# A two-layer encoder on one core: output product of the 1024-token requests in f16 parts, product with V one head later, side work in other slots, loops written out

## The chip, the cores and the metric

One Trainium2 chip, and of it one core. The time is device microseconds of one launch; three runs of the kernel before are given by their median. One further execution was profiled; all rows of the trace are from it, and its times count from the span's start.

## The reference, cut to what matters

Two requests, a prompt of 512 tokens and a sample of 1024, go through the same trunk of two layers with shared weights (`D_MODEL` = 1024, everything in float32). One layer does, for a request:

```python
h = rms_norm(x, g_norm) * (1 + scale) + shift           # scale, shift, gate from Linear(SiLU(c))
q_lat, kv_lat, k_rope, z_a, q_b, k_b, v_b, z_b = split(h @ w_in)
oa = attention(8 heads, q and k of 64 + 32 from q_lat, kv_lat, k_rope; v of 64)     # MLA
ob = attention(8 query heads, 2 key heads of 64, q and k normed per head, axial rotary)   # GQA
out = concat(oa * silu(z_a), ob * silu(z_b)) @ w_out
x = x + gate * out
```

Attention is a full softmax over all tokens of the request. After both layers comes a last RMS norm.

## The kernel before, in words

**Four instances.** The program runs layer 0 for the prompt (q = 0, r = 0), layer 0 for the sample (q = 1, r = 1), then the same for layer 1 (q = 2, 3). The instances of 512 tokens (4 tiles of 128) are called short here, those of 1024 tokens (8 tiles) long. In the code `delay` is 1 for short ones. Every engine has its own program; they meet in counting semaphores alone.

**Key phase.** An instance begins with `key_step`, one for each tile of keys and two to drain: x is loaded by SyncE into the one buffer `xn`, squared and scaled on ScalarE (the root on GpSimd), transposed on TensorE (`h^T0`, `h^T1`), modulated on VectorE into `hT`, multiplied with `Wkv` (`kv`), and the keys and values of the tile are made from it. In a long instance `h` is split into f16 parts (high on ScalarE, low on VectorE in `h_low`) and kept in memory; SyncE issues the store after `h_low` and the next x after `h^T1`. `load_w`, after the first step, brings the f16 parts of the query weights (two transfers). They were made in tiles 2 and 3 of the short instance of the same layer. `Wout` is loaded after the last step, in two transfers, and so is `gate`, one row for all partitions.

**Tiles.** Then each tile of 128 query tokens runs through 16 slots, one for each head: 0 to 7 MLA, 8 to 15 GQA. In slot h TensorE runs `turn(h)` (transposes of the exponentials of head h, L677), `scores(h + 2)` (L695), side work, and `mix`, the product with V (L905). The exponentials are split into f16 parts: ScalarE copies the transposed block to f16 (`move_pt`, L1398), VectorE subtracts to get the low part (L1214), and `mix` adds three products (high with high, high with low, low with high). In short instances `mix(h - 1)` runs in slot h, since two heads fit into `PT`; in long ones `mix(h)` runs in its own slot and waits for `pt_low` of that head. `turn(h)` waits for the exponentials of h and for the low part of head h - 1, whose PSUM banks it writes. ScalarE's order in a slot is `move_pt(h)`, the exponential of h + 1 (L1390), tanh for a z; VectorE's in a long instance is the outputs of a group of heads, low part, side result, row maximum of head h + 2 (L1197), other side results.

**Side work.** The dictionaries `FINISH`, `GATE_A`, `GATE_B`, `PREPARE`, `TURN` and `LEFT_OVER` say which side product runs in which slot, ahead of `mix` (left of the bar) or behind it; "/0" and "/1" are the two halves (four k each) of a product over 1024. For tile i: the gates z_a, z_b of the tile; y_b^T and the output product out0, out1 of tile i - 1; q_lat, q_b, q_up and the transposes of q for tile i + 1; y_a^T of the tile. A side product has one PSUM bank (`SIDE`) in a long instance, two in a short one; it starts when the product before it has been taken out by VectorE (`mm_free`). In `scores` the heads 0, 1, 4 and 8 wait for the latest side result (L695's wait is on `mm_free` of `rounds.now() - later`).

**Output product.** For both lengths `yT` is float32, and out0, out1 are eight float32 matmuls each of 128x512 (`product`, L695) with `Wout`, whose rows GpSimd has multiplied with `gate` in the slots `GATE_SLOTS` of the first tile (`gate_output_weights`). VectorE adds x (L1182). The z and q products of long instances already run as three f16 products (`product3`, L686 to L688).

**Gates.** GpSimd's `gates` turns sums of exponentials and scales into one factor per head and multiplies it into G; for long instances the factor holds `in_unscale` of the f16 products.

**Loops.** In short instances all tiles are written out. In long ones `over_tiles` writes tiles 0 and 7 out and puts tiles 1 to 6 into a hardware loop (`tile_loop`, `Fori`) on every engine, with waits on values from registers; `key_steps` does the same for the steps in the middle. In layer 1 the last norm of tile i - 1 hangs on each tile (`final_square`, `final_rstd`, `final_rows`, L1230), with a load of `g_final` and a store of the result by SyncE.

Of the kernel before, what the change touches and what calls it, by code (L numbers as in the profile page):

```python
# [18 lines left out]
F16 = mybir.dt.float16  # L19
# [67 lines left out]
def slots(first, last, ada):  # L87

    parts = [GATE_B, TURN] + ([ADA] if ada else [])
    if not first:  # L90
        parts += [GATE_A, FINISH]
    else:
        parts.append(LEFT_OVER)
    if not last:
        parts.append(PREPARE)
    return [[[n for p in parts for n in p.get(slot, "|").split("|")[a].split()] for a in (0, 1)]
            for slot in range(2 * HEADS)]
# [7 lines left out]
class Count:  # L105


    def __init__(self):
        self.n, self.over = 0, 0

    def now(self):
        return self.n + self.over
# [4 lines left out]


@contextmanager
def tile_loop(eng, first, end, by=1, **counts):  # L120

    assert (end - first) % by == 0
    with eng.Fori(first, end - by + 1, by) as i:
        at = {k: c.n for k, (c, _) in counts.items()}
        for c, per in counts.values():
            c.over = (i - first) * per
        yield i
        for k, (c, per) in counts.items():
            assert c.n - at[k] == per * by, (k, c.n - at[k], per)
            c.over = 0  # L130
            c.n += per * (end - first - by)


def encoder(nc, x_prompt, x_sample, c_prompt, c_sample, w_ada, b_ada, g_norm, w_in, g_qa, w_uq,
# [20 lines left out]
    with ExitStack() as ctx:  # L155
# [43 lines left out]
        rows1_sb = sb("rows1_sb", [32, P])  # L199
# [5 lines left out]
        w_top = sb("w_top", [P, len(W_CHUNKS)])  # L205
        w_max = sb("w_max", [P, DEPTH])
# [8 lines left out]
        hT_parts = hT[:, 0, :, :].rearrange("p k n -> p (k n)").bitcast(F16).rearrange("p (a k n) -> p a k n", a=2, k=KD)  # L215
        Wq_parts = Wq[:, :, :].rearrange("p k n -> p (k n)").bitcast(F16).rearrange("p (k n) -> p k n", k=KD)

        def w_chunk(j):
            k, n, c, w = W_CHUNKS[j]
            return Wq[:, k:k + n, c:c + w], parts[:, j % 2, :].rearrange("p (k a n) -> p k a n", k=n, a=2)  # L220
        junk = sb("junk", [P, 2 * D], BF16)
# [47 lines left out]

        g_final_rows = [region1[:, 0:D], region2[:, at - D:at]]  # L270
# [40 lines left out]
        def side_bank(S, n):  # L311
# [14 lines left out]
            "h_high", "h_low",  # L326
# [14 lines left out]
        def pt_block(h, S, c):  # L341

            return c + (h % 2 * S // P if 2 * S <= SMAX else 0)
# [17 lines left out]
        def key_steps(eng, NT, per, step, loop_from=2):  # L361


            for i in range(loop_from):
                step(i, i % 2)
            if loop_from < NT - 2:
                with tile_loop(eng, loop_from, NT - 2, by=2, **per) as i:
                    step(i, 0)
                    step(i + 1, 1)
            for i in range(max(loop_from, NT - 2), NT):  # L370
                step(i, i % 2)
            step(NT, 0)
            step(NT + 1, 1)

        def over_tiles(eng, NT, per, tile):

            tile(0, True, False)
            if NT == tiles[0]:
                for i in range(1, NT - 1):
                    tile(i, False, False)  # L380
            else:
                with tile_loop(eng, 1, NT - 1, **per) as i:
# [1305 lines left out]
```

## Time and profile before

| | us |
|---|---|
| median of three runs | 2509.02 |
| lowest, highest | 2506.0, 2953.74 |
| the profiled execution, its own time | 2508.32 |
| its span, first to last instruction | 2506.5 |
| TensorE matmul busy | 2243.5 (90%) |
| VectorE busy | 1405.4 (56%) |
| ScalarE busy | 971.3 (39%) |
| GpSimd busy | 798.9 (32%) |
| mean granted TensorE clock | 0.958 |

Busy time is the union of an engine's instructions; matmul ends are modelled and overlap the next one's start, so the pace of TensorE is better read from starts in the chain than from mean durations. The chain of the work that ended last follows each step back to what released it; "issue" in it is time in which the engine waited for nothing that the profile shows. A float32 matmul of 512 columns stands in the trace as two records. The two layers' long instances run from about 450 to 1250 and from about 1640 to 2506 us.

### The profile page before, as it was taken

How to read it: one execution, taken by the hardware profiler on the slowest of the kernel's cores; microseconds unless marked ns; L12 is line 12 of the kernel's file. 1: busy time of each engine (PE TensorE's matmuls, PEld its weight loads, DVE VectorE, ACT ScalarE, POOL GpSimd, SP SyncE). 2: the span in 40 equal slices, each digit the busy share in tenths (PEclk: the TensorE clock that was granted, in tenths of full speed). 3: DMA queues.
4: the chain of work that ended last, by engine and by line, in shares of the span. 5: the costliest groups of instructions: out<-in, count | busy, mean ns of one | idle time of the engine just before them, and what ended most of it. 6: DMA issues, size and time to landing. Idle time of an engine off the chain costs nothing.

```text
span 2506.5 us, 44027 instructions
## 1 busy us (share of the span) xinstructions
PE 2243.5 (90%) x16426; PEld 1343.1 (54%) x16426; DVE 1405.4 (56%) x2342; ACT 971.3 (39%) x2174; POOL 798.9 (32%) x1311
## 2 busy tenths in 40 slices
PE   3888998699999999999988899868998988988997
PEld 1445554355666666666544555435565655655664
DVE  3546565375665556565544655547565555545563
ACT  0123344233544444444412334422453443434452
POOL 0553231375332123112155323147532212203210
PEclk7899999799999999999999999989999999999999
DMA  9712134430000000000521001363000000010001
GB/s 297 273 43 68 59 110 163 176 151 10 18 18 8 25 17 25 8 25 17 192 94 67 18 35 71 119 232 136 10 18 27 10 35 27 9 35 27 9 26 42
DMA packets 75965, 172.29 MB, mean 69 GB/s; under 512 B 7586, under 2 KB 34312, under 8 KB 75292
## 3 DMA queue, kind: packets, MB, share of 16 engines
q1 hardware_dynamic: 75808, 170.03, 19.0%
q8 instruction: 118, 1.93, 0.3%
q14 instruction: 39, 0.32, 0.0%
HBM read 130.12 MB, written 39.90 MB: 68 GB/s over the span
## 4 chain that ended last, share of the span: by engine, by line
PE 71%; DVE 14%; issue 5%; DMA 3%; ACT 3%; POOL 2%; SPq 2%; DVEq 0%; POOLq 0%; ACTq 0%
PE psum L695 41%; PE psum L677 11%; PE psum L905 6%; DVE region L1214 4%; PE psum L686 4%; PE psum L688 4%; PE psum L687 4%; DVE nmax L1197 3%; DVE hT L1009 1%; DMA xn<-x_after_layer 1%; DMA xn<-in_x_sample 1%; POOL region L1451 1%; ACT region L1398 1%; ACT region L1374 1%; DVE region L1172 1%
## 5 line engine op out<-in xcount | busy, mean ns | idle before, releaser
L1398 ACT ACTIVATE region<-psum 128x512 f16<-128x512 f32 x640 | 354.0, 594 | 708.8 <-PE psum L677 708.7
L1214 DVE TENSOR_TENSOR region<-psum,region 128x512 f16<-128x512 f32 x640 | 416.8, 684 | 301.9 <-ACT region L1398 301.3
L677 PE MATMUL psum<-ident,region 128*128 128x128 f32 (+1 forms) x3208 | 445.2, 280 | 59.1 <-issue 35.1
L677 PEld LDWEIGHTS psum<-ident,region 128*128 128x128 f32 (+1 forms) x3208 | 364.4, 142 | 126.8 <-issue 92.2
L1197 DVE TENSOR_REDUCE nmax<-psum 128x1 f32<-128x1024 f32 (+1 forms) x384 | 399.1, 1039 | 56.2 <-PE psum L695 55.4
L695 PE MATMUL psum<-Wout,region 128*128 128x512 f32 x768 | 352.3, 604 | 3.9 <-DVE region L1182 1.6
L695 PE MATMUL psum<-KTa,region 96*128 96x512 f32 x640 | 323.5, 622 | 24.6 <-DVE region L1172 13.1
L1451 POOL TENSOR_TENSOR rsum<-sums,v_scale 128x8 f32<-128x8 f32 x48 | 13.1, 273 | 812.3 <-ACT region L1390 812.3
L1451 POOL TENSOR_TENSOR region<-region,rope_sb 128x64 f32<-128x64 f32 (+3 forms) x384 | 159.4, 436 | 308.7 <-DVE region L1168 293.6
L1390 ACT ACTIVATE region<-psum,nmax,unscale 128x1024 f32<-128x1024 f32 (+1 forms) x192 | 204.4, 1064 | 136.0 <-DVE nmax L1200 135.2
L1390 ACT ACTIVATE region<-psum,nmax 128x1024 f32<-128x1024 f32 (+1 forms) x192 | 186.9, 973 | 113.3 <-DVE nmax L1197 112.3
L695 PEld LDWEIGHTS psum<-Wout,region 128*128 128x128 f32 x768 | 143.4, 193 | 157.1 <-issue 145.2
L695 PE MATMUL psum<-Wq,hT 128*128 128x512 f32 (+1 forms) x512 | 204.6, 547 | 7.9 <-DMA hT<-h_transposed 6.5
L905 PEld LDWEIGHTS psum<-Vb,region 128*128 128x128 f16 x3840 | 138.9, 99 | 122.2 <-DVE region L1214 49.5
L905 PEld LDWEIGHTS psum<-Va,region 128*128 128x128 f16 x3840 | 136.3, 98 | 112.1 <-DVE region L1214 69.4
L686 PE MATMUL psum<-Wq,hT 128*128 128x512 f16 (+1 forms) x512 | 181.3, 354 | 6.7 <-DMA hT<-h_transposed 6.7
L905 PE MATMUL psum<-Vb,region 128*128 128x64 f16 x3840 | 154.9, 195 | 31.2 <-DVE region L1214 15.9
L687 PE MATMUL psum<-Wq,hT 128*128 128x512 f16 (+1 forms) x512 | 181.2, 354 | 0.0
L688 PE MATMUL psum<-Wq,hT 128*128 128x512 f16 (+1 forms) x512 | 181.1, 354 | 0.0
L695 PE MATMUL psum<-region,hT 128*128 128x416 f32 x384 | 153.1, 556 | 22.0 <-DVE hT L1009 19.4
L695 PE MATMUL psum<-KTb,region 128*128 128x512 f16 x640 | 170.8, 381 | 1.2 <-DVE region L1158 1.2
L695 PEld LDWEIGHTS psum<-KTa,region 96*128 96x128 f32 x640 | 112.5, 198 | 105.0 <-issue 85.5
(132 smaller groups left out, 2518.9 us busy)
## 6 DMA issues: line engine op xcount, KB each, us to landing
Wout<-in_w_out SPq DMA_DIRECT2D x8, 2048.0 KB, 9.7
w_in_parts<-parts SPq DMA_DIRECT2D x28, 512.0 KB, 3.2
Wq<-w_in_parts SPq DMA_DIRECT2D x4, 3584.0 KB, 18.4
Va<-in_w_ada SPq DMA_DIRECT2D x12, 1024.0 KB, 5.7
Wq<-in_w_in SPq DMA_DIRECT2D x6, 2048.0 KB, 14.1
hT<-h_transposed SPq DMA_DIRECT2D x24, 512.0 KB, 3.3
h_transposed<-parts SPq DMA_DIRECT2D x16, 512.0 KB, 2.7
Wq<-in_w_ada SPq DMA_DIRECT2D x3, 2048.0 KB, 13.2
```

The costliest lines, as they stand in the source:

```text
L677: return nc.tensor.transpose(out, in_, ident[0:n, 0:n])
L686: nc.tensor.matmul(out, hT_parts[:, 0, k, :], high(k), start=k == 0, stop=False)
L687: nc.tensor.matmul(out, hT_parts[:, 0, k, :], low(k), start=False, stop=False)
L688: last = nc.tensor.matmul(out, hT_parts[:, 1, k, :], high(k), start=False, stop=k == KD - 1)
L695: last = nc.tensor.matmul(out, lhsTs[k], rhss[k], start=k == 0, stop=k == n - 1)
L905: last = nc.tensor.matmul(out, PT[:, a, pt_block(h, S, c), :], v, start=c == 0 and a + b == 0, stop=c == NT - 1 and a == 1)
L1009: last = nc.vector.tensor_scalar(hT[:, odd, k, :], ps[:, j * P:(j + 1) * P], gs[:, m, k:k + 1], cols[:, 16 * m + k:16 * m + k + 1], ALU.mu ...
L1197: last = nc.vector.reduce_max(nmax[:, h:h + 1], scores_buf(h, S), AX_X, negate=True)
L1214: nc.vector.tensor_tensor(PT[:, 1, pt_block(h, S, 4 * c):pt_block(h, S, 4 * c) + 4, :], psum[:, T_BANK + b, :].rearrange("p (c n) -> p c n ...
L1390: nc.scalar.activation(probs_buf(h, S), scores_buf(h, S), ACT.Exp, bias=nmax[:, h:h + 1], scale=scale, accum_out=sums[:, h:h + 1]).then_in ...
L1398: nc.scalar.activation(PT[:, 0, pt_block(h, S, 4 * c):pt_block(h, S, 4 * c) + 4, :], psum[:, T_BANK + b, :].rearrange("p (c n) -> p c n", ...
L1451: mul = lambda out, a, b: nc.gpsimd.tensor_tensor(out, a, b, ALU.mult)
```

## The change

- Long instances: `Wout`, once multiplied with `gate`, is scaled by a power of two and split into f16 parts in the first tile (high on ScalarE in `output_weights`, low on VectorE in its own `output_weights`, then a transfer from `parts` to `Wout_parts` by SyncE, `keep_out`). `y` gets a scale per token from the largest |G| of its row (`token_bound`, after z_a and z_b); GpSimd puts the scale into its factor, y^T is split into two f16 parts on VectorE, out0 and out1 are `product3`, and VectorE's addition of x undoes the scale. The scales come from `output_scales`, after slot 0 of the first tile, and from maxima over `Wout` that VectorE takes in the first eight slots of the short instance; GpSimd's gating there waits for each.
- Long instances: `mix(h - 1)` in slot h, with a second buffer `PT_next` for every other head, and one `mix` behind the last tile. VectorE's outputs of a group move behind low part, side result and maximum.
- Both lengths: new slots. z_b, out0, out1 one later, q_lat^T from 9 to 8, q_a^T0 and q_a^T1 at 13 and 14, y_a^T from 14 to 15, and q_b^T of a tile at slot 5 of that tile, not at slot 15 of the one before. `scores` of heads 0, 4, 8, 12 wait for the transposes they read, by name.
- The parts of the query weights and `Wout` of a long instance come in pieces of one k, two after each key step (`load_parts`); the last two of `Wout` after the last step.
- `tile_loop` is gone: all tiles and key steps of all instances are written out.

```diff
-FINISH = {2: "y_b^T |", 10: "| out0/0", 11: "out0/1 |", 12: "| out1/0", 13: "out1/1 |"}
+FINISH = {2: "y_b^T |", 11: "| out0/0", 12: "out0/1 |", 13: "| out1/0", 14: "out1/1 |"}
 GATE_A = {0: "| z_a/0", 1: "z_a/1 |"}
-GATE_B = {2: "| z_b/0", 3: "z_b/1 |"}
-PREPARE = {6: "q_lat |", 7: "| q_b/0", 8: "q_b/1 |", 9: "q_lat^T | q_up0",
-           10: "q_up1 |", 12: "q_a^T0 |", 14: "q_a^T1 |", 15: "q_b^T0 | q_b^T1"}
-TURN = {14: "| y_a^T"}
-
-LEFT_OVER = {5: "| q_b^T0@0 q_b^T1@0"}
+OWN = {3: "| z_b/0", 4: "z_b/1 |", 5: "q_b^T0 | q_b^T1", 15: "| y_a^T"}
+PREPARE = {6: "q_lat |", 7: "| q_b/0", 8: "q_b/1 | q_lat^T", 9: "q_up0 |", 10: "q_up1 |", 13: "q_a^T0 |", 14: "| q_a^T1"}
...
+            if 2 * S <= SMAX:
+                return PT[:, a, c + h % 2 * S // P:, :]
+            return (PT, PT_next)[h % 2][:, a, c:, :]
...
+        def over_tiles(NT, tile):
+
+            for i in range(NT):
+                tile(i, i == 0, i == NT - 1)
...
+                for k in (2 * t, 2 * t + 1):
+                    if k < KD:
+                        sp.dma_start(Wq_parts[:, k, :], w_kept[l][:, k, :]).then_inc(s["w_parts_loaded"], 16)
+                    elif k < 2 * KD - 2:
+                        sp.dma_start(Wout[:, k - KD, :], w_out[l][(k - KD) * P:(k - KD + 1) * P, :]).then_inc(s["wout_loaded"], 16)
+
+            def keep_out(k):
+                sp.wait_ge(s["out_low"], KD * l + k + 1)
+                sp.dma_start(Wout_parts[:, k, :], parts[:, k % 2, :]).then_inc(s[f"out_moved{k % 2}"], 16)
...
+                            if half != "1" and c == 0 and i == 0:
+                                for odd in (0, 1):
+                                    pe.wait_ge(s[f"out_moved{odd}"], 16 * KD // 2 * (l + 1))
+                            last = product3(ps, yT_parts, lambda k: Wout_parts[:, k, c * BANK:(c + 1) * BANK],
+                                            lambda k: Wout_parts[:, k, D + c * BANK:D + (c + 1) * BANK], half)
...
-                    if h in (0, 1, 4, 8):
-                        pe.wait_ge(s["mm_free"], rounds.now() - later)
+                    if h % 4 == 0:
+                        pe.wait_ge(s["mm_free"], at[("q_a^T0", "q_a^T1", "q_b^T0", "q_b^T1")[h // 4]])
...
-                        if h or delay == 0 or not first:
-                            mix(h - delay, i)
+                        if h or not first:
+                            mix(h - 1, i)
...
+                    if i == 0 and h < KD:
+                        if h == 0:
+                            dve.wait_ge(s["wout_loaded"], wout_loaded(q))
+                        nc.vector.tensor_reduce(out_top[:, h:h + 1], Wout[:, h, :], AX_X, ALU.max, apply_absolute_value=True) \
+                            .then_inc(s["out_top_local"], 1)
...
+                def output_scales():
+
+                    dve.wait_ge(s["x_out_moved"], 16 * (b0 + q + 1))
+                    then(nc.vector.tensor_reduce(out_bound[:, 0:1], gate, AX_X, ALU.max, apply_absolute_value=True))
...
+                    nc.vector.tensor_tensor(out_unscale[:, l:l + 1], out_bound[:, 0:1], in_unscale[:, l, 0:1], ALU.mult) \
+                        .then_inc(s["out_scales"], 1)
...
+                    if h - 2 in GATE_SLOTS:
+                        k = GATE_SLOTS.index(h - 2)
+                        dve.wait_ge(s["out_high"], KD * l + k + 1)
+                        nc.vector.scalar_tensor_tensor(out=parts[:, k % 2, D:2 * D], in0=Wout[:, k, :], scalar=out_scale[:, l:l + 1],
+                                                       in1=parts[:, k % 2, 0:D], op0=ALU.mult, op1=ALU.subtract) \
+                            .then_inc(s["out_low"], 1)
...
+                        then(nc.vector.tensor_reduce(y_bound[:, 1:2], half, AX_X, ALU.max, apply_absolute_value=True))
+                        then(nc.vector.tensor_scalar(y_bound[:, 0:1], y_bound[:, 0:1], y_bound[:, 1:2], 1e-30, ALU.max, ALU.max))
+                        nc.vector.tensor_scalar(y_bound[:, 0:1].bitcast(U32), y_bound[:, 0:1].bitcast(U32),
+                                                0x7F800000, None, ALU.bitwise_and).then_inc(s["y_bounded"], 1)
...
+                            then(nc.vector.tensor_copy(high, blocks))
+                            last = nc.vector.tensor_tensor(low, blocks, high, ALU.subtract)
...
+                    if r and name in ("z_a", "z_b"):
+                        dve.wait_ge(s["mm_free"], rounds.now())
+                        if i == 0 and name == "z_b":
+                            token_bound(0)
+                        token_bound(int(name == "z_b"))
...
+                            move_pt(h, i)
+                            for name in names[:early]:
+                                side(name, owner(name, i))
+                            next_max(h, i, last)
                         if h == HEADS:
                             outputs(0, i)
                         if h == 0 and not first:
                             outputs(1, i - 1)
-                        if not delay:
-                            move_pt(h, i)
-                            for name in names[:early]:
-                                side(name, owner(name, i))
-                            next_max(h, i, last)
...
+                    if h - 1 in GATE_SLOTS:
+                        k = GATE_SLOTS.index(h - 1)
+                        if k == 0:
+                            act.wait_ge(s["out_scales"], l + 1)
+                        if k < 2:
+                            act.wait_ge(s[f"h_stored{k}"], 8 * (b0 + NT))
+                        wait(act, f"out_moved{k % 2}", 16 * (KD // 2 * l + k // 2))
+                        act.wait_ge(s["out_gated"], KD * l + k + 1)
+                        nc.scalar.activation(parts[:, k % 2, 0:D], Wout[:, k, :], ACT.Copy, scale=out_scale[:, l:l + 1]) \
+                            .then_inc(s["out_high"], 1)
...
+                        pool.wait_ge(s["out_top_local"], KD * l + k + 1)
                     last = mul(Wout[:, k, :], Wout[:, k, :], gate)
-                    if k == KD - 1:
+                    if r:
+                        last.then_inc(s["out_gated"], 1)
...
+                        pool.wait_ge(s["y_bounded"], kept_before[q] + i + 1)
+                        if i == 0:
+                            pool.wait_ge(s["out_scales"], l + 1)
+                        mul(y_unscale[:, i % 2:i % 2 + 1], y_bound[:, 0:1], out_unscale[:, l:l + 1])
+                        then(mul(y_scale[:, :], y_bound[:, 0:1], v_unscale[:, l:l + 1]))
                     then(mul(inv, sums[:, 8 * a:8 * a + 8], v_scale2[:, q, a:a + 1].broadcast_to([P, HEADS])))
+                    if r:
+                        then(mul(inv, inv, y_scale[:, 0:1].broadcast_to([P, HEADS])))
```

## Rows read from the trace of the kernel before

**Rows 1.** The page, the chain that ended last: shares of the span by engine.
```profile
PE 71%; DVE 14%; issue 5%; DMA 3%; ACT 3%; POOL 2%; SPq 2%; DVEq 0%; POOLq 0%; ACTq 0%
```

**Rows 2.** Busy time by stretch; columns PE, PEld, DVE, ACT, POOL, granted clock, DMA share, GB/s.
```profile
586.35:662.31 75.96, 70.22 (x688) 47.48 (x686) 49.50 (x71) 38.81 (x84) 37.01 (x37) 0.96 0.05 15
662.31:1176.65 514.34, 510.64 (x4430) 320.46 (x4429) 301.86 (x439) 238.42 (x505) 124.53 (x174) 1.00 0.05 19
1769.92:1842.74 72.82, 67.05 (x687) 44.96 (x686) 49.14 (x71) 38.74 (x84) 37.43 (x37) 1.00 0.05 16
1842.74:2317.97 475.23, 437.03 (x3692) 274.06 (x3691) 258.83 (x371) 204.94 (x432) 107.25 (x155) 0.95 0.07 24
2317.97:2404.87 86.90, 85.41 (x740) 53.56 (x739) 51.10 (x74) 40.84 (x86) 21.45 (x31) 1.00 0.04 15
```

**Rows 3.** Chain (start, us, what), the fifth turn of layer 1's loop.
```profile
2305.87 7.02 issue
2312.89 1.87 PE psum L677 x8
```

**Rows 4.** Chain, a turn of layer 0's loop.
```profile
831.26 1.00 PE psum L677 x8
```

**Rows 5.** Chain, layer 0: half an output product, and one f16 matmul of a z product.
```profile
800.94 3.52 PE psum L695 x8
...
834.68 0.22 PE psum L686
```

**Rows 6.** Waits of weight loads, six middle tiles of layer 0: total us, times, longest.
```profile
PEld psum L905 <- DVE region L1214: 22.8, 65, 0.7
```

**Rows 7.** VectorE's instructions by line and form: xcount, busy us, mean ns, idle before.
```profile
L1214 DVE TENSOR_TENSOR region<-psum,region 128x512 f16<-128x512 f32 x640 | 416.8, 684 | 301.9 <-ACT region L1398 301.3
...
L1197 DVE TENSOR_REDUCE nmax<-psum 128x1 f32<-128x1024 f32 x256 | 311.6, 1217 | 36.3 <-PE psum L695 36.0
...
L1094 DVE SCALAR_TENSOR_TENSOR parts<-Wq,in_scale,parts 128x1024 f16<-128x1024 f32 x28 | 37.9, 1352 | 0.0
...
L1083 DVE TENSOR_REDUCE w_top<-Wq 128x1 f32<-128x1024 f32 x28 | 33.8, 1208 | 0.0
```

**Rows 8.** Waits of TensorE, first tile of layer 0's long instance.
```profile
PE psum L695 <- DVE region L1174: 1.9, 1, 1.9
PE psum L695 <- DVE region L1172: 1.8, 1, 1.8
```

**Rows 9.** GpSimd in order of time, the same tile: next tile's rotation, then Wout's eighth row.
```profile
634.40 1.83 POOL L1451 TENSOR_TENSOR region<-region,rope_sb 128x128 f32<-128x128 f32 x4 [6.47 <-DVE region L1168]
...
648.38 2.34 POOL L1451 TENSOR_TENSOR Wout<-Wout,region 128x1024 f32<-128x1024 f32 x1
```

**Rows 10.** SyncE's issues in order of time, key phase of layer 0's long instance.
```profile
465.36 1.21 SPq L448 DMA_DIRECT2D Wq<-w_in_parts  x2
```

**Rows 11.** Chain, the same phase.
```profile
472.28 17.83 DMA xn<-in_x_sample
```

**Rows 12.** TensorE in order of time, the same phase: three key products.
```profile
475.21 5.85 PE L695 MATMUL psum<-region,hT 128*128 128x416 f32 x16 [0.50 <-DVE hT L1009]
...
500.05 5.75 PE L695 MATMUL psum<-region,hT 128*128 128x416 f32 x16
...
509.93 5.85 PE L695 MATMUL psum<-region,hT 128*128 128x416 f32 x16 [0.28 <-DVE hT L1009]
```

**Rows 13.** DMA issues: xcount, KB each, median us from issue to landing.
```profile
Wq<-w_in_parts SPq DMA_DIRECT2D x4, 3584.0 KB, 18.4
...
hT<-h_transposed SPq DMA_DIRECT2D x24, 512.0 KB, 3.3
...
xn<-in_x_sample SPq DMA_DIRECT2D x8, 512.0 KB, 3.7
```

**Rows 14.** Waits of TensorE, first tile of layer 1's short instance.
```profile
PE psum L681 <- POOL region L1597: 3.7, 1, 3.7
```

**Rows 15.** The page, DMA queues: packets, MB, share of 16 engines.
```profile
q8 instruction: 118, 1.93, 0.3%
```

More of the change, by code:

```diff
@@ L359, in key_names, with key_steps @@
             return [name for name, _, _ in key_rounds(i, NT)]
-        def key_steps(eng, NT, per, step, loop_from=2):
-            for i in range(loop_from):
+        def key_steps(NT, step):
+            for i in range(NT + 2):
                 step(i, i % 2)
[L366 to L382, printed above, removed]
-                    tile(i, False, False)
-            tile(NT - 1, False, True)
+        def over_tiles(NT, tile):
+            for i in range(NT):
+                tile(i, i == 0, i == NT - 1)
         def owner(name, i):
-            if "@" in name:
-                return int(name.split("@")[1])
             return i - 1 if name in EPILOGUE else i + 1 if name in PROLOGUE else i
@@ L394, in heads, with wout_loaded @@
             return 16 * (b0 + i) + h + 1
-        PROLOGUE = ["q_lat", "q_b", "q_lat^T", "q_up0", "q_up1", "q_a^T0", "q_a^T1", "q_b^T0", "q_b^T1"]
+        PROLOGUE = ["q_lat", "q_b", "q_lat^T", "q_up0", "q_up1", "q_a^T0", "q_a^T1"]
         EPILOGUE = ["y_b^T", "out0", "out1"]
+        def wout_loaded(q):
+            return sum(16 * (KD if p % 2 else 2) for p in range(q + 1))
         def w_stored(l, j):
@@ L590, in side @@
                     nonlocal last_z_b
-                    name = name.split("@")[0]
                     n = rounds.step()
@@ L856, in side, with scores @@
                     if half != "1":
-                        free = 1 if delay and not between and name != "q_up0" else between
+                        free = 1 if short and not between else between
                         pe.wait_ge(s["mm_free"], rounds.now() - free)
-                    last = query_product(name.split("@")[0], owner(name, i), psum[:, side_bank(S, rounds.now()), :], half)
+                    last = query_product(name, owner(name, i), psum[:, side_bank(S, rounds.now()), :], half)
                     if half != "0":
                         last.then_inc(s["mm_ready"], 1)
-                        rounds.step()
-                def scores(h, i, later):
+                        at[name] = rounds.step()
+                def scores(h, i):
                     out = scores_buf(h, S)
                     wait(pe, "exp_done", heads(b0, i, h - 2))
-                    if h in (0, 1, 4, 8):
-                        pe.wait_ge(s["mm_free"], rounds.now() - later)
+                    if h % 4 == 0:
+                        pe.wait_ge(s["mm_free"], at[("q_a^T0", "q_a^T1", "q_b^T0", "q_b^T1")[h // 4]])
                     j = h - HEADS
@@ L904, in mix @@
                             v = Va[:, c, b, head, :] if head < HEADS else Vb[:, c, b, g * GD:(g + 1) * GD]
-                            last = nc.tensor.matmul(out, PT[:, a, pt_block(h, S, c), :], v, start=c == 0 and a + b == 0,
+                            last = nc.tensor.matmul(out, pt(h, S, a, c)[:, 0, :], v, start=c == 0 and a + b == 0,
                                                     stop=c == NT - 1 and a == 1)
@@ L1176, in query_out @@
                         a = int(name == "y_b^T")
-                        last = nc.vector.tensor_copy(yT[:, 4 * a:4 * a + 4, :], blocks)
+                        if r:
+                            high, low = (yT_parts[:, part, 4 * a:4 * a + 4, :] for part in (0, 1))
+                            then(nc.vector.tensor_copy(high, blocks))
+                            last = nc.vector.tensor_tensor(low, blocks, high, ALU.subtract)
+                        else:
+                            last = nc.vector.tensor_copy(yT[:, 4 * a:4 * a + 4, :], blocks)
                     else:
@@ L1404, in tile @@
                     for h, names in enumerate(schedule):
-                        if not delay:
+                        if not short:
                             move_pt(h, i)
```

246 lines of the change are left out of this document (136 added, 110 removed).

## The prediction, made before the changed kernel ran

> **What bounds the kernel now.** I read first the page's chain: TensorE carries 71% of what ended last, VectorE 14% [rows 1]. Then the table by stage [rows 2]. In the long instance of layer 0, six tiles (first V product of tile 1 to that of tile 7) take 514.34 us, 85.72 each, and TensorE is busy for 510.64 of them at full clock: these tiles are bound by the sum of TensorE's instructions. In layer 1 the same tiles take 475.23 for five, 95.05 each, at a mean granted clock of 0.95, and the sixth 86.90. So something costs 8 us a tile that isn't work, five times. The chain at the turn from one tile to the next shows it [rows 3]: 7.02 us of "issue" (no semaphore, DMA or engine explains it) ahead of the transposes, and then transposes at 1.87 us that take 1.00 at the same place in layer 0 [rows 4], 1.2 instead of 2.4 GHz after the idle. Last I read what the first tile, the key phase and the short instances wait for; these rows come with their steps.
>
> **The sum is made against the profiled execution, 2508.32 us** (span 2506.5 and 1.8 around it), 0.7 below the median 2509.02 of the three runs.
>
> **1. Loops written out.** The five stalls stand where the loop body of layer 1 jumps back (tile 6 to 7 falls through). 95.05 - 86.90 = 8.15, times 5 = 41 us gone. Layer 0's loop turns without a stall, so nothing is gained there. Its bound above: the sixth tile is still 1.2 over layer 0's, the final norm's work at the tile's end. Its VectorE step is now after a transpose with more cover; I take 4 of 6 x 1.2 us.
> The Trainium skill (Runtime: NRT & Kernel Launch, Instruction fetch mechanics) says that a taken branch whose target is outside the fetched window stalls for a fetch, and that sequential crossings are mostly hidden. Layer 1's turn agrees; layer 0's turn, 1.00 us, shows that a body of the same matmuls can also turn freely. If crossings weren't hidden, the written-out code would pay at each one, which is the rival R4.
>
> **2. Output product.** One half (four k) is 3.52 us in float32; a matmul in f16 of the same 512 columns takes 0.22 [rows 5], in the z products 12 to a half: 2.60. Of the 3.52 some 0.09 is the change of operand, which stays, so I take 0.85 x 4 halves = 3.4 us a tile (at most 3.7). 16 tiles of the two long instances: 54 us, all on TensorE's path.
>
> **3. V one head later.** In the six tiles the weight loads of the V product wait 22.8 us for the low part (65 waits, 3.8 a tile) [rows 6], but matmuls already queued cover most: TensorE idles 3.7 us out of 514.34 by busy time. Between 0 and 3.8 a tile I take 1.6: 12 x 1.6 = 19. First and last tiles have less side work and more such waits; I take 2.5 for each first and 3 for each last: 11. Together 30.
>
> **4. New waits in a middle tile.** VectorE takes 0.68 us for a pass over 512 columns of PSUM (half a low part, z, a transposed result) and 1.22 for a row maximum [rows 7]. Its order within a slot is low part, side result, maximum. Added are two maxima over 512 gate columns (0.6 each, half of the 1.21 for 1024 [rows 7]) and two more 0.68 for the low parts of y^T: 2.6 us, against 35 us idle a tile ((514.34 - 301.86) / 6 [rows 2]), so only the order counts. Slot by slot with these durations and TensorE's: after z_b (now slot 4) come ScalarE's tanh, z, the token maximum, two tiny steps, then the row maximum that the next exponential waits for. The low part in slot 5 and the first q_b^T result queue behind it, and TensorE may not start the second q_b^T until that result leaves the one side bank: 1.4 us late. q_up0 needs q_lat^T out, which is behind q_b, a maximum and the outputs: 0.9. In slot 13 out1 waits for q_a^T0's result behind a low part: 0.6. z_a: 0.2. Sum 3.1 a tile, 12 tiles: +37 (0 if VectorE's overlaps absorb them, 75 if each also pulls its neighbour).
> GpSimd's three small extra steps a tile and its wait for the bound stand beside an engine idle for three quarters of the tile [rows 2]: nothing, and ScalarE needs their result eight slots later.
>
> **5. First tile of a long instance.** Gone: the scores no longer wait for the transposes just issued, 1.9 + 1.8 [rows 8], and layer 0's two half-clock stretches (75.96 against 72.82 [rows 2]), 2 x 3.7 + 2 = 9.5. Added: eight low-part splits of Wout on VectorE, 1.35 each [rows 7], half of them in slots that VectorE ends: 4. Ten dependent steps for the scales after slot 0, one of them over 1024 columns, which hold up the low part of slot 1: 3 (a choice; no row shows such a series). The z_b chain with an extra maximum: 1. And one queue: ScalarE's eighth split waits in slot 13 for GpSimd's eighth gated row, which stands behind the next tile's rotations. From q_up1's result that takes 634.40 to 650.7, 16.3 us [rows 9]; ScalarE gets there 11 us after it, so exponentials and copies queued behind it come 4 us late. 12.5 x 2 = 25, net +15.5 (V's gain is in step 3; between -4 and +30). The eight moves of the parts have a whole tile before slot 11 of tile 1 asks for them: nothing. Last tiles: +1 for both.
>
> **6. Loads in the key phase.** Now two transfers of 3.6 MB of weight parts go out at 465.36 [rows 10, 13], and the next x behind them takes 17.83 us to land [rows 11] instead of 3.7 [rows 13]; from one key product to the next it takes 24.84 us there and 9.88 in the step after [rows 12]: 15.0 lost, once in each long instance. New: two blocks of 0.92 MB in each of four steps, two of 0.5 MB in three. They go out just before the next x, which still stands behind them. From 465.36 to x's landing at 490.11 the queue moved 8.4 MB, parts and two transfers of 0.5, in 24.75 us: 5.4 us for two blocks. An x that lands in 3.7 and is ready 3.4 later (490.1 to 493.5 in that step) has some 2 us in hand in a step of 9.9, so the first pays over 3; a stretched step gives the blocks more of a lead over the next x, so they pay by turns, and I take 1.2 a step, 5 in all. 15 less 5 is 10 saved in each of two phases: 20 (0 if each x pays in full, 30 if none).
> The Trainium skill (DMA: Bandwidth & Descriptors, Queues, rings and completion order) says that an engine takes descriptors in ring order. This speaks against the spreading: the bytes ahead of the x loads are the same. The 17.83 agrees with it. By the rule alone the gain would be 0 to 20; without it 30.
> The gate and Wout land earlier than before. The next h loads after z_b, a slot later than before; it has slot 5 (over 3.5 us) for a transfer of 3.3 [rows 13]: nothing in long tiles, up to 1 in short.
>
> **7. Short instances.** First tile: eight maxima over Wout of 1.21 us on VectorE in its first eight slots, some 3.5 us in each. Gone: q_b^T at the tile's end, which in one tile waits 3.7 for GpSimd [rows 14] and less in the others. With the later z_b: -7 for both. Written-out key steps: nothing.
>
> **Sum:** -41 - 4 - 54 - 30 + 37 + 15.5 + 1 - 20 - 7 = -102.5, so 2508.3 - 102.5 = 2406.
>
> **Rivals.**
> R1, VectorE's order takes back the product's gain: middle tiles stay at layer 0's 85.7 (no gain of 1.9 each, 12 x 1.9 = 23) and first tiles lose 12 more. TensorE's clock would drop after waits of 2 us, as it did in the first tile of layer 0 (0.96 [rows 2]). 2440. For: q_b^T beside z_b on one bank. Against: 35 us of idle a tile. 0.20.
> R2, the new waits are absorbed: 2406 - 37 = 2369. For: today's busy share of 99% with V unlagged. 0.15.
> R3, the change doesn't do what it says at the turn: the 7 us come from the final norm's transfers, which only layer 1 has there. 2406 + 41 = 2447. Against: the sixth tile has them too and takes 86.90 [rows 2]. 0.05.
> R4, slower than before: written-out code stalls where it is fetched. The instruction queue moved 118 packets [rows 15] for at most 9,036 matmuls of program text plus 3,695 of layer 1's loop, some 7 a tile; layer 0's loop, now free, pays too. 12 tiles x 7 = 84 fetches. It decides from 1.2 us a fetch (102.5 / 84); at half a turn, 3.5, the time is 2406 + 294 = 2700. Against: the first long tiles are straight code, and their long waits name an engine [rows 8]. 0.03.
> My forecast: 0.55. The 0.02 left goes to cases not named.
>
> **How the numbers follow.** 2406 is the forecast. The low end takes R2 and part of step 6: 2355. The high end takes R1, R3 and the upper bound of step 5: 2455. Two per cent either side of 2509 (what a run can tell) is 2459 to 2559. Under it lie the forecast, R1, R2, R3 but for their tails: faster 0.91, same 0.06, slower 0.03.
>
> **What would show it.** The turns of layer 1 at 1 us and its middle tiles within 2 us of layer 0's; 48 f16 output matmuls a tile at 0.22; no V weight load waiting for the low part; waits of about 1 us behind q_b^T and q_lat^T; ScalarE waiting for GpSimd late in the first tile; x landing within 10 us in the key phase. Middle tiles over 86 us, or "issue" gaps in straight code, would make it wrong.

## The result and the profile after

The changed kernel takes **2409.51 us** (median of four runs, 2407.04 to 2411.33) against 2508.24 for the kernel before (median of four). One of those four took 2953.74; the ratio leaves it out (2507.46) and is 0.9609, 95% interval 0.9590 to 0.9627. 2406 was forecast. The profiled execution took 2407.04, span 2405.0 against 2506.5. The sum is right to 4 us; the table shows that two of its terms aren't.

I split both traces at the first score product that each tile's slot 0 runs (head 2), which stands at the same place of the program in both. "Forecast" is the prediction's terms put on the same stages.

| Stage | before | after | difference | forecast |
|---|---|---|---|---|
| start to the first tile | 146.2 | 146.1 | -0.1 | 0 |
| short instances, tiles 0 to 2 | 422.3 | 400.1 | **-22.2** | -7 |
| short last tiles, key phases of the long instances | 438.4 | 418.8 | -19.5 | -20 |
| first tiles of the long instances | 148.8 | 178.1 | **+29.4** | +10.5 |
| six middle tiles, layer 0 | 514.3 | 500.2 | -14.1 | -11.4 |
| six middle tiles, layer 1 | 561.1 | 500.2 | -60.9 | -56.4 |
| last tiles, drains, key phase of layer 1's short instance | 275.4 | 261.4 | -14.0 | -18.6 |
| sum | 2506.5 | 2405.0 | -101.5 | -103 |

(+10.5 is the net 15.5 of step 5 less 5 of V; -18.6 is four output products of 3.4, 6 of V and 1 back.) The first tiles cost 19 us more than forecast, the short instances gained 15 more; every other stage is off by less than 5.

The table by stage of the changed kernel, first V product of tile 0 to tile 1 and of tile 1 to tile 7, for both layers (columns as in [rows 2]):

```profile
566.15:661.33 95.18, 76.10 (x704) 50.34 (x702) 68.06 (x91) 47.55 (x93) 40.14 (x38) 0.91 0.15 56
661.33:1161.52 500.19, 484.98 (x4525) 314.35 (x4524) 319.03 (x474) 237.87 (x504) 126.55 (x186) 1.00 0.06 20
1722.53:1816.59 94.06, 74.98 (x703) 49.84 (x702) 67.99 (x91) 47.53 (x93) 40.21 (x38) 0.93 0.15 57
1816.59:2316.78 500.19, 484.96 (x4525) 314.32 (x4524) 325.76 (x480) 244.08 (x516) 130.82 (x198) 1.00 0.08 27
```

Layer 0's 514.34 [rows 2] are 500.19, and layer 1's tiles take the same to the hundredth: nothing is left of the turns, and the clock is 1.00. The first tiles grew, and their granted clock fell to 0.91 and 0.93.

The chain at a turn of layer 1 (start, us, what; four transposes of y and the eight of the turn), then half an output product in layer 0, first and last of its twelve matmuls and what follows, then slot 13, where the next half starts late:

```profile
2138.67 1.35 PE psum L665 x12
2140.02 1.72 PE psum L683 x4
```

```profile
876.38 0.22 PE psum L674
...
878.76 0.22 PE psum L676
878.98 0.87 PE psum L665 x8
...
885.47 1.19 DVE PT_next L1263 x2
886.66 0.61 DVE region L1207
887.27 0.05 issue
887.32 0.39 PE psum L674
```

No "issue" stands at the turn, and its transposes run at 0.11 each; compare [rows 3]. The half product takes 878.98 - 876.38 = 2.60 us, as forecast, for 3.52 [rows 5]. The last lines are the forecast's wait in slot 13: the result that frees the bank (L1207, q_a^T0) stands on VectorE behind a low part.

TensorE's waits in layer 0's six middle tiles (total us, times, longest):

```profile
PE psum L669 <- DVE region L1209: 8.5, 6, 1.4
PE psum L674 <- DVE region L1207: 2.5, 6, 0.4
PE psum L683 <- DVE region L1201: 1.3, 6, 0.2
PE psum L665 <- ACT region L1457: 1.2, 6, 0.2
```

Row by row: the second q_b^T behind the first, 1.4 a tile; out1 behind q_a^T0; q_up0 behind q_lat^T; the turn. Of the 22.8 us that weight loads waited for a low part [rows 6], 1.4 are left.

The first tile of layer 0: TensorE's waits, ScalarE's, VectorE's series for the scales of Wout and GpSimd beside it (both in order of time):

```profile
PE psum L665 <- ACT region L1457: 7.9, 1, 7.9
PE psum L665 <- DVE PT_next L1263: 7.7, 3, 6.2
```

```profile
ACT parts L1419 <- POOL Wout L1520: 8.6, 1, 8.6
```

```profile
566.44 0.15 DVE L1104 TENSOR_SCALAR out_scale<-out_bound 128x1 f32<-128x1 f32 x1
566.63 1.29 DVE L1105 TENSOR_TENSOR out_bound<-v_scale 128x1 f32<-128x1 f32 x1
567.95 0.16 DVE L1106 RECIPROCAL v_unscale<-out_bound 128x1 f32<-128x1 f32 x1
568.15 2.07 DVE L1107 SCALAR_TENSOR_TENSOR out_bound<-out_bound,v_unscale 128x1 f32<-128x1 f32 x1
570.25 2.26 DVE L1109 TENSOR_TENSOR out_unscale<-out_bound,in_unscale 128x1 f32<-128x1 f32 x1
572.43 1.27 DVE L1263 TENSOR_TENSOR PT_next<-psum,PT_next 128x512 f16<-128x512 f32 x2
```

```profile
563.24 9.26 POOL L1520 TENSOR_TENSOR Wout<-Wout,region 128x1024 f32<-128x1024 f32 x4
```

Two waits make up most of the tile's loss: 6.2 of TensorE's 7.7 us stand in slot 1 behind the low part that VectorE began at 572.43, after the series; 7.9 stand in slot 14 behind ScalarE, which waited 8.6 us for GpSimd's eighth row of Wout (the forecast's queue). In the series five steps on one column take 0.15 to 0.21, but three take 1.29, 2.07 and 2.26. GpSimd multiplies four rows in the same time, 2.31 each, so they end at about 565.6, 567.9, 570.2 and 572.5; the three slow steps end at 567.92, 570.22 and 572.51.

### The profile page after: what moved, and what is told of

It reads as the page before. It is cut to its first block, busy times and chain, and to the rows that moved or that the text cites. A ratio compares the mean times of both kernels' runs of the same rounds, so it can differ in the third digit from the quotient of the medians.

```text
span 2405.0 us, 41364 instructions
## 1 busy us (share of the span) xinstructions
PE 2150.7 (89%) x16682; PEld 1314.9 (55%) x16682; DVE 1501.1 (62%) x2490; ACT 986.8 (41%) x2190; POOL 808.8 (34%) x1343
## 4 chain that ended last, share of the span: by engine, by line
PE 65%; DVE 20%; DMA 4%; ACT 4%; POOL 3%; issue 2%; SPq 2%; DVEq 0%; POOLq 0%; ACTq 0%
PE psum L683 31%; PE psum L665 10%; PE psum L674 6%; PE psum L676 6%; PE psum L675 6%; PE psum L901 5%; DVE nmax L1246 4%; DVE PT_next L1263 2%; ACT region L1457 1%; DVE region L1263 1%; DVE hT L1002 1%; POOL region L1520 1%; DVE region L1198 1%; ACT region L1441 1%; DMA xn<-x_after_layer 1%
## 5 line engine op out<-in xcount | busy, mean ns | idle before, releaser
L1263 DVE TENSOR_TENSOR region<-psum,region 128x512 f16<-128x512 f32 x384 | 251.6, 682 | 158.3 <-ACT region L1465 158.1
L1465 ACT ACTIVATE region<-psum 128x512 f16<-128x512 f32 x384 | 214.7, 593 | 312.1 <-PE psum L665 311.4
L683 PE MATMUL psum<-KTa,region 96*128 96x512 f32 x640 | 312.5, 604 | 5.3 <-DVE region L1207 5.3
L1465 ACT ACTIVATE PT_next<-psum 128x512 f16<-128x512 f32 x256 | 139.1, 594 | 275.3 <-PE psum L665 275.3
L1263 DVE TENSOR_TENSOR PT_next<-psum,PT_next 128x512 f16<-128x512 f32 x256 | 164.0, 682 | 34.2 <-ACT PT_next L1465 33.3
L1343 ACT ACTIVATE junk<-region 128x64 bf16<-128x64 f32 (+3 forms) x300 | 87.6, 299 | 190.9 <-DVE region L1160 71.0
L1198 DVE SCALAR_TENSOR_TENSOR region<-region,psum 128x512 f32<-128x512 f32 x48 | 33.0, 687 | 199.9 <-ACT region L1441 199.9
L683 PEld LDWEIGHTS psum<-Wq,hT 128*128 128x128 f32 x512 | 95.7, 195 | 87.3 <-issue 70.8
```

Source lines behind the costliest of these rows:

```text
L683: last = nc.tensor.matmul(out, lhsTs[k], rhss[k], start=k == 0, stop=k == n - 1)
L1263: nc.vector.tensor_tensor(pt(h, S, 1, 4 * c)[:, 0:4, :], psum[:, T_BANK + b, :].rearrange("p (c n) -> p c n", c=4), pt(h, S, 0, 4 * c)[:, ...
L1343: return nc.scalar.activation(junk[:, at:at + n], row, ACT.Square, scale=float(n) ** -0.5, accum_out=stat_col)
L1465: nc.scalar.activation(pt(h, S, 0, 4 * c)[:, 0:4, :], psum[:, T_BANK + b, :].rearrange("p (c n) -> p c n", c=4), ACT.Copy).then_inc(s["pt_ ...
```

## The experiments

Times are medians, ratios against the kernel before beside each. Line numbers shift by a few between versions.

**Loops written out, nothing else.**

```diff
-                with tile_loop(eng, 1, NT - 1, **per) as i:
-                    tile(i, False, False)
+            for i in range(1, NT - 1):
+                tile(i, False, False)
...
```

> The kernel before with its loops written out and nothing else. If the five stalls belong to the jump back (my step 1), the six middle tiles of layer 1 take layer 0's 514 us in place of 561, everything else keeps its time, and the run takes 2461 us. If they come from the final norm's transfers (R3), they stay: 2508. If written-out code stalls where it is fetched (R4), there are new gaps without a releaser in TensorE's row and the time is above 2508.

2464.59 us, ratio 0.9839 (0.9810 to 0.9867): 40.4 less than the kernel before beside it (2505.02). Layer 1's six middle tiles by the table by stage, and the page's row of the instruction queue:

```profile
1839.53:2360.84 521.31, 512.36 (x4430) 320.40 (x4428) 308.18 (x445) 243.72 (x518) 128.82 (x186) 1.00 0.07 24
```

```profile
q8 instruction: 131, 2.15, 0.4%
```

521.31 for 562.13 in [rows 2] (475.23 and 86.90): 40.8 gone, and 7 (1.2 a tile) still over layer 0's. The stall was the loop's (R3 falls). The queue moved 131 packets, 13 more than with loops [rows 15], and no new gap appeared in straight code (R4 falls). The same queue tells the two loops apart: in the kernel before it moved nothing in tiles 2 to 6 of layer 0 (760.5 to 1175 us) and 46 packets in tiles 1 to 5 of layer 1 (1841.1 to 2315 us); written out, the six middle tiles of layer 1 take 35.

**Scales from steps with one SBUF tensor.**

```diff
-then(nc.vector.tensor_tensor(out_bound[:, 1:2], v_scale[:, m, 0:1], v_scale[:, m, 1:2], ALU.min))
+then(nc.vector.tensor_scalar(out_bound[:, 1:2], v_scale[:, m, 0:1], v_scale[:, m, 1:2], None, ALU.min))
...
```

> The changed kernel; of the nine steps that make the scales of Wout on VectorE, the three that read two tensors from SBUF (1.29, 2.07 and 2.26 us for one column) read one tensor and a per-partition scalar instead, with the same result. Theory: these three wait for the row of Wout that GpSimd is multiplying (each ends when one of GpSimd's rows ends), because the two engines share a way to SBUF. Then the series falls from 7.9 us to about 3, TensorE's wait in slot 1 from 6.4 to about 1.5 with no half clock behind it, and each first long tile gains about 7: 2395 us. Rival: a dependent step simply costs this much, or the releaser of slot 1 is another: no change, 2409.

2393.55 us, ratio 0.9555 (0.9527 to 0.9583). VectorE in order of time, the same steps:

```profile
567.10 0.21 DVE L1105 TENSOR_SCALAR out_bound<-v_scale 128x1 f32<-128x1 f32 x1
567.35 0.16 DVE L1106 RECIPROCAL v_unscale<-out_bound 128x1 f32<-128x1 f32 x1
567.54 0.21 DVE L1107 TENSOR_SCALAR out_bound<-out_bound,v_unscale 128x1 f32<-128x1 f32 x1
567.79 0.21 DVE L1109 TENSOR_SCALAR out_unscale<-out_bound,in_unscale 128x1 f32<-128x1 f32 x1
567.92 1.28 DVE L1263 TENSOR_TENSOR PT_next<-psum,PT_next 128x512 f16<-128x512 f32 x2
```

Each of the three takes 0.21; the series falls from 7.9 to 2.9 us (565.03 to 567.92). The first tiles fall from 89.6 and 88.5 to 82.3 and 82.5: 7.3 and 6.0; in layer 0, 1.4 of it is the half clock (1.2 GHz) in slot 2, where the changed kernel's transposes start 0.22 us apart and not 0.11. The rival that such a step simply costs this much fails in the changed kernel's own trace, where GpSimd is idle beside the same operation on one column of two SBUF tensors:

```profile
292.35 0.23 DVE L1066 SCALAR_TENSOR_TENSOR in_unscale<-in_bound 128x1 f32<-128x1 f32 x2
```

Two of them take 0.23. The theory holds: the time was GpSimd's rows.

**GpSimd's last rows of Wout earlier.**

```diff
-        GATE_SLOTS = [3, 4, 5, 6, 8, 9, 11, 12]
+        GATE_SLOTS = [3, 4, 5, 6, 8, 9, 10, 11]
```

> The changed kernel with GpSimd's seventh and eighth row of Wout (and the splits that follow them) one and two slots... that is, in slots 10 and 11 and not 11 and 12, so that the eighth stands ahead of the next tile's rotations. Theory: ScalarE's 8.6 us wait in the first long tile goes, with TensorE's 8.2 behind it and the half clock after it: about 9 us in each of two tiles, 2391 us. Rival: the rotations, now 2.3 us later, hold the transposes of q, and half of it comes back: 2400.

2390.67 us, ratio 0.9543 (0.9516 to 0.9571). The first tiles fall by 7.2 and 6.9, not 9, so only 14 of the 18.8 us are the theory's, and that the total is the forecast one is luck. In layer 0 slots 14 and 15 give back 8.5 and 2.1, and slot 12 takes 2.4, by a third mechanism that neither theory had: ScalarE waits longer for the moves that free the two buffers of the parts, 4.1 us in this tile of the changed kernel and 7.4 here (ScalarE's waits):

```profile
ACT parts L1419 <- DMA Wout<-parts: 7.4, 3, 3.5
```

**V in its own slot, twice.** First only the place of the product; then also VectorE's outputs of a group of heads ahead of the low part, as before the change.

```diff
-                        if h or not first:
+                        if not short:
+                            mix(h, i)
+                        elif h or not first:
                             mix(h - 1, i)
```

> The changed kernel with the product with V of head h again in slot h in the long instances (the second buffer stays). My step 3: the lag is worth 1.6 us in a middle tile, 2.5 in a first and 3 in a last one, so middle tiles go from 83.4 to 85 and the run to about 2439 us. Rival A: the waits were covered by queued work, the lag is worth nothing: 2409. Rival B: with the new order the uncovered waits are all of 3.8 a tile: 2465.

2540.28 us, ratio 1.0141 (1.0111 to 1.0170): 131 us over the changed kernel, beyond even the rival. Middle tiles of layer 0 take 89.4 to 92.7. TensorE's waits in that instance:

```profile
PE psum L901 <- DVE region L1274: 28.5, 12, 2.8
PE psum L901 <- DVE PT_next L1265: 6.5, 12, 0.9
```

The largest is V's wait for the outputs (L1274), which the change had moved behind the low part: the new order needs the lag. Whether the lag needs the new order, no run shows. So the second run:

```diff
+                        if h == HEADS:
+                            outputs(0, i)
                         if not short:
                             move_pt(h, i)
```

> As the run with V in its own slot, but VectorE also takes the outputs of a group of heads first in a slot again, as in the kernel before, so that the lag alone is undone. That run lost 7.7 us in a middle tile, 5.6 of it in slots 0 and 8, where the outputs are taken; if these are the order's, what is left is 2.1 us a tile (my step 3 said 1.6): middle tiles of 85.5, in all about 2442 us. Rival: the lag itself is worth more, and the outputs in front only move the loss to the low part behind them: above 2480.

2470.71 us, ratio 0.9859 (0.9826 to 0.9891), 70 us less than the first run. In layer 0 every middle tile is 1.81 us longer than the changed kernel's, the last 3.2: step 3 said 1.6 and 3. In layer 1 five of the six are 5.9 to 7.3 longer, which no theory had; the time is in slot 0 (VectorE in order of time there):

```profile
2004.54 1.27 DVE L1281 SCALAR_TENSOR_TENSOR region<-region,rinv 128x1024 f32<-128x1024 f32 x1
2007.33 0.69 DVE L1274 TENSOR_TENSOR region<-psum,region 128x512 f32<-128x512 f32 x1 [1.51 <-POOL region L1522]
2007.94 1.28 DVE L1265 TENSOR_TENSOR region<-psum,region 128x512 f16<-128x512 f32 x2
```

The last norm's step (L1281) and the outputs, which wait for GpSimd (L1522), stand ahead of the low part that V needs.

**Parts of the weights in one go.**

```diff
-                for k in (2 * t, 2 * t + 1):
...
+                    for k in range(KD):
+                        sp.dma_start(Wq_parts[:, k, :], ...
```

> The changed kernel with the f16 parts of the query weights all issued after the first key step, and Wout after the last, eight pieces each. My step 6: 10 us lost again in each of two key phases, 2429 us, with one x that takes about 18 us to land. If only the bytes ahead of the x loads count, whatever their place in the queue, nothing changes: 2409. If the pieces now cost nothing: 2439.

2442.41 us, ratio 0.9746 (0.9714 to 0.9777). The chain in the key phase, of the changed kernel and of this run:

```profile
466.10 6.67 DMA xn<-in_x_sample
...
477.49 7.69 DMA xn<-in_x_sample
```

```profile
460.44 18.16 DMA xn<-in_x_sample
```

From the third to the eighth key product layer 0 takes 64.09 us here, 64.50 before and 54.27 in the changed kernel: step 6's ten (7.3 in layer 1). The other eight of layer 0's 18.1 lost in this phase (15.4 in layer 1) are not step 6: this run puts all of Wout ahead of the h load that the first query product waits for, 12.2 us instead of 6.8; 3 stay unexplained.

**q_b^T of the short instances back in slot 15.**

```diff
+LATE = {15: "q_b^T0 | q_b^T1"}
+OWN_SHORT = {3: "| z_b/0", 4: "z_b/1 |", 15: "| y_a^T"}
```

> The changed kernel; in the short instances alone q_b^T of the next tile stands in slot 15 again (with y_a^T behind it), and slot 5 has it only in the first tile. Theory: the 22 us that the short instances gained come from there, since GpSimd's rotations end after slot 15 begins; 3 to 5 us come back in each of six tiles: 2430. Rival: the gain is from the other moved slots (z_b, the output product): 2409.

2427.89 us, ratio 0.9688 (0.9653 to 0.9722). TensorE's waits at the end of the first tile of layer 1's short instance:

```profile
PE psum L678 <- POOL region L1679: 6.1, 1, 6.1
```

In layer 0 the same wait is 4.3; the changed kernel has neither. The first tiles lose 8.0 and 8.5, the others between -1.5 and 0.9: the theory is right for first tiles alone, 16.5 of the 22 us. That two tiles of 8 come near the total forecast from six of 3 to 5 is luck, and what gave the other 6 us stays open.

**Three edits together** (the scales, GpSimd's rows in slots 2 to 9, q_b^T1 moved):

```diff
-... 5: "q_b^T0 | q_b^T1", 15: "| y_a^T"}
+... 5: "q_b^T0 |", 6: "| q_b^T1", 15: "| y_a^T"}
-        GATE_SLOTS = [3, 4, 5, 6, 8, 9, 11, 12]
+        GATE_SLOTS = [2, 3, 4, 5, 6, 7, 8, 9]
```

> The changed kernel with three edits: the scales from steps with one SBUF tensor; GpSimd's rows of Wout in slots 2 to 9; q_b^T1 behind V in slot 6, no longer beside q_b^T0 in slot 5 on the one side bank. From the runs so far 7 a first tile for the scales (13), 9 for the rows (18), and if the 1.6 us of slot 5 are TensorE's wait for the first q_b^T's result, 1.3 in each of 16 long tiles (20): 2358 us. Rival: the wait only moves (to q_lat in slot 6 or q_b in slot 7, on the same bank): 2378. Second rival: rows two slots earlier meet VectorE's own two-tensor steps and give half of their 18 back.

2368.83 us, ratio 0.9450 (0.9426 to 0.9474). The first tiles get 15.5 and 15.6 shorter, the 31 us expected; the two runs by themselves had given 27. Moving q_b^T1 gives 0.49 a middle tile, not 1.3: most of the wait moves, as the first rival has it, though not to a product on the side bank. TensorE's waits in five middle tiles, where the row of L1209 (7.1) is gone and that of the turn behind ScalarE's exponential has grown from 1.0:

```profile
PE psum L665 <- ACT region L1457: 5.3, 10, 0.9
```

The run has a fourth edit: SyncE waits for one score product more before it loads the next instance's key weights. In layer 0's last short tile that wait is 6.8 us where it was 3.9, ScalarE then waits 3.7 us for a store of the query weights' parts where it waited 0.6, and the tile is 3.8 longer; this edit wasn't run alone.

**The token's bound behind the row maximum.**

```diff
                             next_max(h, i, last)
+                            bound(names[:early], i)
```

> The changed kernel; VectorE takes the token's bound (one maximum of 0.69 us and two tiny steps, 1.15 in all) behind the next row maximum and no longer ahead of it, after z_a and after z_b. My step 4: everything ahead of the low part and of the first q_b^T result delays the second q_b^T, so moving these 1.15 us... they stay ahead of both and TensorE's 1.6 us in slot 5 stay; z_a's slot gains at most 0.4: 2405 to 2409. Rival: the row maximum waits for the late bound, the exponential for it, and slot 5 falls to about 0.5: 16 tiles by 1.1, 2392.

2402.24 us, ratio 0.9589 (0.9543 to 0.9635), which can't be told from the changed kernel's; the trace can: 0.51 a middle tile, 0.39 of it in the slot behind z_a's second half and 0.13 in slot 5. The time is a little under the range expected, 2405 to 2409, since slot 5 gives something too. VectorE there, from z_b's result to the second q_b^T's bank:

```profile
843.99 0.69 DVE L1198 SCALAR_TENSOR_TENSOR region<-region,psum 128x512 f32<-128x512 f32 x1 [3.63 <-ACT region L1445]
844.59 1.22 DVE L1249 TENSOR_REDUCE nmax<-psum 128x1 f32<-128x1024 f32 x1
845.72 0.68 DVE L1127 TENSOR_REDUCE y_bound<-region 128x1 f32<-128x512 f32 x1
846.43 0.21 DVE L1128 TENSOR_SCALAR y_bound<-y_bound 128x1 f32<-128x1 f32 x1
846.68 0.15 DVE L1129 TENSOR_SCALAR y_bound<-y_bound 128x1 uint32<-128x1 uint32 x1
846.75 1.28 DVE L1266 TENSOR_TENSOR PT_next<-psum,PT_next 128x512 f16<-128x512 f32 x2
847.95 0.68 DVE L1209 CAST region<-psum 128x512 f16<-128x512 f32 x1
```

VectorE works through without a gap. For slot 5 it is the sum of what is ahead that counts, not the order among it: bound and row maximum change places and only 0.13 of the 1.6 goes.

**The last four pieces of Wout behind the h load**, on top of the three:

```diff
                 load_h(0)
+                if r:
+                    for k in range(KD - 4, KD):
+                        sp.dma_start(Wout[:, k, :], ...
```

> The run with three edits, and the last four pieces of Wout issued behind the h load at the end of the key phase. In the changed kernel that h load stands behind 2 MB of Wout and takes 6.8 us where it took 3.3, TensorE waits 6.8 for it. By the order of the queue it lands in 3.3 again: 3.5 us in each of two key phases, 2362. Rival: the product waits for its weights then, or GpSimd's first rows for Wout: 2369 as before.

2363.29 us, ratio 0.9435 (0.9393 to 0.9477): the fastest version run, though its interval overlaps that of the three. TensorE's wait for h, in the changed kernel and here:

```profile
PE psum L674 <- DMA hT<-h_transposed: 6.8, 1, 6.8
```

```profile
PE psum L673 <- DMA hT<-h_transposed: 3.7, 1, 3.7
```

And the stretch that holds its first long tile (559.93 to 632.57), with the clock at 1.00:

```profile
558.00:640.00 82.00, 73.83 (x715) 49.24 (x715) 66.69 (x97) 52.18 (x100) 45.89 (x43) 1.00 0.17 65
```

## Why the prediction was right, and where it wasn't

**Step 1 (turns) held**: 40.4 us by the run with nothing else, 41 forecast, and R4 fell with it: the trace shows no new gap in straight code. The Trainium skill (Runtime: NRT & Kernel Launch, Instruction fetch mechanics) says that sequential crossings are mostly hidden, and the 35 packets without a stall agree. The last norm's 1.2 a tile went entirely in the changed kernel, about 7 us where I took 4.

**Step 2 (output product) held**: 2.60 a half, and TensorE's own work in a middle tile is 3.36 less, 3.4 forecast.

**Step 3 (V) held in size in layer 0**, 1.81 in a middle tile and 3.2 in the last, but not as an edit that stands alone: undone by itself it costs 131 us, and 70 of them come back when the outputs too go to their old place. I hadn't costed the move of the outputs at all, nor named what covers it; the lag is the cover. What the lag alone is worth in layer 1 isn't shown, since the run without it loses 5.9 to 7.3 there beside the last norm.

**Step 4 (new waits) held.** Time over TensorE's own work rose by 1.0 a middle tile. With V's 1.8 gone the new waits are 2.8, forecast 3.1. They stand in the slots named: slot 5 1.6 (1.4 forecast), slots 8 and 9 0.9 (0.9), slot 13 0.6 (0.6), behind z_a 0.4 (0.2). R2 falls with this: its tiles would take 80.7 (85.7 - 3.4 - 1.6), not 83.4. Of R1 one half falls, since middle tiles didn't stay at 85.7, and the other, dearer first tiles with half clock in them, came true by another mechanism.

**Step 5 (first long tile) is the step that failed.** The stage came out 19 us above the forecast; with the 3.6 that V gives there (1.4 and 2.2 in the run without the lag) the step's own net is 33, past its upper bound of 30. Two of its terms were mis-sized. "Ten dependent steps for the scales ... 3 (a choice; no row shows such a series)" is at least 7: the run with one-tensor steps takes 7.3 and 6.0 out of a tile. I counted steps and not what they read. A step of VectorE with two tensors in SBUF stood until GpSimd's running row ended, and GpSimd had four rows in a line there because nothing in its queue made it wait. The Trainium skill (SBUF — State Buffer, Who interferes with whom) says that a VectorE instruction with two SBUF inputs contends with a GpSimd instruction that reads SBUF, and that the ports they share are an exclusive lock. The trace agrees: 2.26 us against 0.21 for the same result with one tensor. I hadn't held that rule against the new series. The second term, ScalarE behind GpSimd's eighth row, was the right mechanism at the wrong price: 4 forecast, and 8.6 of waiting measured, 8.5 in slot 14 and 2.1 in slot 15 with the half clock. The stretch from the first rotation to the end of that row takes 18.6 us (621.40 to 640.05), not 16.3, and ScalarE is there after 10.2, not 11. The 2.3 more are three of GpSimd's steps, 1.44, 1.42 and 1.71 us where they took 0.46, 1.04 and 0.73, each beside one of VectorE's new splits of Wout, which read two SBUF tensors: the same contention, the other way round. The moves of the parts, which I put at nothing because their results are wanted a tile later, also hold up ScalarE by 4.1 us for their two buffers. In the sum itself 4, 3, 1 and 4 are 12 a tile and not 12.5, which is 1 us of 15.5. With better places for the rows, one-tensor steps and q_b^T1 moved, 15.5 a tile come back.

**Step 6 (key phase) held, and missed a queue.** The spreading saves 10.2 us a phase, 10 forecast, and the order of the queue shows in how: each x still stands behind the pieces, 6.67 and 7.69 us against 3.7 [rows 13], but a step of 9.8 covers most of that, and five steps lose 5.3 (54.27 less five of 9.8) where one x lost 15. What I missed is what the earlier Wout stands ahead of: 2 MB of it now go out before the h load, which takes 6.8 us instead of 3.3, and the last run gets this back.

**Step 7 (short instances) was 15 us too cautious.** I took the wait on GpSimd as its row showed it, 3.7 in one tile. With what it pulled along (the copy, the scores behind it, half clock) it costs 8.0 and 8.5 in the two first tiles by the run that brings it back, where the waits themselves are 4.3 and 6.1.

So 2406 against 2409.5 is two misses of opposite sign, +19 and -15, around terms that were right to within 5 us a stage. The runs bear out the other mechanisms; that the total is right to 4 us is luck.

## What to carry to other kernels

A series of tiny dependent steps is priced by what each reads and who else is reading then, not by its count: with GpSimd busy on SBUF, give VectorE one tensor and a per-partition scalar. A wait's row in a table of waits is the least that it costs; read the excess of the whole slot and the next ones. Undo one edit of a change alone only after asking which other edit of it was made possible by it, or the run prices both.

## What the runs showed of the hardware

The three steps above: 1.29, 2.07 and 2.26 us for one column beside GpSimd's rows, 0.21 each without the second SBUF tensor, and two of the kind in 0.23 with it when GpSimd is idle. It goes both ways: GpSimd's step L1544 on 128x256 takes 0.73 us in 22 of its 24 places in the changed kernel and 1.71 in the two, one in each layer, where a split of Wout on VectorE had begun just before (in layer 0 at 633.33, GpSimd's step at 633.69).

And two loops with the same matmuls: layer 0's turned without a stall [rows 4] and without a packet of program in tiles 2 to 6; layer 1's lost 6.9 to 7.2 us at each of its five turns (7.02 in [rows 3]) and moved 46 packets in its five tiles. All of it written out moved 13 more packets than before and lost nothing. Why layer 0's body turned freely stays open.
